# Last attention tiles reordered, the slots' second half skipped between narrow experts, and a copy in place of a dummy scatter

## The reference, cut to what matters

```python
u = rms_norm(h, norm1_g)
proj = u @ w_in
conv_out = conformer_conv_group(proj[..., :c0], conv_w, conv_b, conv_ln_g, conv_ln_b)
attn_out = swa_sink_attention(q, k, v, q_norm_g, k_norm_g, sinks)
h = h + concatenate([conv_out, attn_out], axis=-1) @ w_out
v = rms_norm(h, norm2_g).reshape(B * S, D)
h = h + moe_top4_of_32(v)      # sum of gate * (clamped_swiglu(v @ w1 + b1) @ w2 + b2)
```

## Time and profile before

| what | value |
|---|---|
| median of 3 runs | 1993.06 us (1991.5 to 1994.81) |
| profiled execution, its own time | 1994.85 us |
| its span in the trace | 1993.1 us |
| mean granted TensorE clock | 0.992 |
| PE busy | 1925.4 us, 97% of the span |
| DVE busy | 1010.1 us, 51% |
| ACT busy | 449.9 us, 23% |
| POOL busy | 415.6 us, 21% |
| bytes moved by DMA | 513.21 MB, 258 GB/s |

### The profile page before, as it was taken

How to read it: one execution, slowest core, us unless ns; L and a number is a source line. 1 busy time by engine, 2 the same in 40 slices (tenths; PEclk the granted TensorE clock), 3 DMA queues, 4 the chain that set the end, 5 groups by cost and what they waited for, 6 DMA issues and landing times.

```text
span 1993.1 us, 35237 instructions
## 1 busy us (share of the span) xinstructions
PE 1925.4 (97%) x12983; PEld 1589.3 (80%) x12984; DVE 1010.1 (51%) x2627; ACT 449.9 (23%) x983; POOL 415.6 (21%) x410
## 2 busy tenths in 40 slices
PE   5999989989999999999999999999999999999996
PEld 3545545457888877888887888999999999999996
DVE  2989973354555545555554555444444444443332
ACT  3166565111111111111111111222222211211111
POOL 3111100011222222222232222222222222221211
PEclk9999999999999999999999999999999999999998
DMA  7000033538999999999999999999888899887651
GB/s 242 1 1 1 6 112 136 186 114 293 349 343 332 352 338 350 351 341 332 351 339 351 351 347 331 313 323 311 303 301 302 304 308 308 298 294 244 223 181 40
DMA packets 237153, 513.21 MB, mean 258 GB/s; under 512 B 11085, under 2 KB 15721, under 8 KB 237104
## 3 DMA queue, kind: packets, MB, share of 16 engines
q1 hardware_dynamic: 215408, 448.89, 62.6%
q0 software_dynamic: 19840, 63.23, 11.9%
q10 hardware_dynamic: 1856, 0.41, 0.1%
HBM read 479.30 MB, written 33.19 MB: 257 GB/s over the span
## 4 chain that ended last, share of the span: by engine, by line
PE 91%; DVE 4%; ACT 2%; issue 1%; DMA 1%; POOL 0%; SPq 0%; ACTq 0%; DVEq 0%; POOLq 0%
PE bank L1175 50%; PE bank L1219 12%; PE bank L1194 12%; PE bank L1392 5%; PE bank L1267 4%; DVE arena L932 2%; PE bank L1303 2%; PE bank L1314 1%; PE bank L1207 1%; PE bank L1553 1%; PE bank L1208 1%; PE bank L1342 1%; DMA arena<-in_x 1%; PE bank L1259 0%; PE bank L1366 0%
## 5 line engine op out<-in xcount | busy, mean ns | idle before, releaser
L1175 PE MATMUL bank<-arena 128*128 128x128 f32 (+5 forms) x8192 | 1000.7, 284 | 6.9 <-issue 6.1
L1175 PEld LDWEIGHTS bank<-arena 128*128 128x128 f32 x8192 | 986.5, 191 | 18.8 <-issue 17.8
L377 POOL DMA_INDIRECT arena<-token_rows,idx_q x256 | 250.1, 977 | 649.0 <-PE bank L1175 589.1
L808 DVE TENSOR_SCALAR arena<-bank,b1c 128x256 f32<-128x256 f32 x256 | 123.4, 482 | 407.2 <-PE bank L1175 407.2
L497 ACT ACTIVATE arena<-arena 128x256 f32<-128x256 f32 x256 | 106.6, 417 | 853.9 <-DVE arena L808 853.9
L1219 PE MATMUL bank<-arena 128*128 128x512 f32 x576 | 250.2, 592 | 0.0
L1194 PE MATMUL bank<-arena 128*128 128x144 f32 (+4 forms) x1792 | 246.8, 293 | 3.0 <-ACT arena L501 2.9
L1194 PEld LDWEIGHTS bank<-arena 128*128 128x128 f32 x1792 | 235.3, 190 | 6.2 <-ACT arena L501 6.2
L383 POOL DMA_INDIRECT out<-arena,idx_cur x64 | 99.4, 1553 | 535.9 <-DVE arena L865 492.1
L1219 PEld LDWEIGHTS bank<-arena 128*128 128x128 f32 x576 | 108.1, 190 | 129.1 <-issue 129.1
L932 DVE SCALAR_TENSOR_TENSOR arena<-arena,cols 128x512 f32<-128x512 f32 (+1 forms) x226 | 182.3, 807 | 12.5 <-ACT arena L592 5.5
(11 more groups left out here) (229 smaller groups left out, 1102.4 us busy)
## 6 DMA issues: line engine op xcount, KB each, us to landing
arena<-in_w SPq DMA_DIRECT2D x192, 2048.0 KB, 12.6
arena<-in_b SPq DMA_DIRECT2D x32, 512.0 KB, 12.7
arena<-in_x SPq DMA_DIRECT2D x16, 512.0 KB, 6.4
token_rows<-arena SPq DMA_DIRECT2D x8, 576.0 KB, 3.2
out<-arena SPq DMA_DIRECT2D x8, 512.0 KB, 6.0
arena<-token_rows,idx_q POOLq DMA_INDIRECT x256
arena<-in_w_in SPq DMA_DIRECT2D x2, 1536.0 KB, 13.1
arena<-in_w_in SPq DMA_DIRECT2D x1, 3072.0 KB, 19.5
```

What stands on the lines that cost most here:

```text
L377: pool.indirect_dma_start(out=gath_q[:, g, :], out_offset=None, in_=quads_d, in_offset=bass.IndirectOffsetOnAxis(ap=idx_q[:, g:g + 1], axis=0)
L808: v.tensor_scalar(g1[:, r, :], bank[r][:, 0:SLOTS], b1c[:, m:m + 1], LIMIT, ALU.add, ALU.min).then_inc(g1_ready, 1)
L1175: last = mm(bank[m % 2][:, side * SLOTS:side * SLOTS + n], w1_sb[:, k, lo:lo + P], xT[:, k, 0:n], start=k == 0, stop=k == KD - 1)
```

## The change

**VectorE and ScalarE, last attention tiles.** In tile 6 the groups of taps go from 8, 4 and (behind the q normalization) 4 to 5, 7 and 0; the four taps taken away stay for the end, so the last group has nine taps and not five. In tile 7 `deviation(0)` goes from ahead of `softmax_a(6)` to behind the two-count group of taps, and `rescale(0)` from ahead of `softmax_b(6)` to behind it. Behind the last tile `softmax_b(7)` goes ahead of `deviation(1)`. ScalarE does `take_PT(6)` ahead of `swish(0)`, and `take_PT(7)` ahead of `swish(1)` in round t = 0 where it was in round 1.

**TensorE, last attention tiles.** In tile 7 `trans_q(7)` goes ahead of two of the four variance sums and two of the three mean sums; the second side of `out_half(0, 0)` goes behind `trans_p(6)`; `trans_p(7)` goes ahead of `turn_rows(0)` and `out_half(1, 1)`, with its wait on bank 5 changed from `vt_ev` to `cen_done`; `turn_rows(0)` side 1 gets a wait for `take_PT(7)`.

**Expert passes.** Where this pass and the next are narrow, `slots_to_tokens` does one half only. For that the narrow body is there twice on TensorE: a loop over 17 passes with one half and one pass with two. The codes move from bank 6 to bank 2 behind column 256. The second half of the codes keeps its earlier value, and the gathers still run by it. In a narrow pass the dummy indirect add on POOL becomes a plain DMA of 2 x 16 floats to a scratch tensor.

```diff
 # POOL, end of a pass
                 with pool.If(over < 1):
-                    add_rows(pool, 1, zeros)
+                    pool.dma_start(spare_d, zeros[:, 0:QW]).then_inc(added[1], 16)
 # ScalarE
                 if s + 1 < NT:
                     take_q(s + 1)
-                else:
-                    swish(0)
                 if s >= 1:
                     take_PT(s - 1)
+                if s == NT - 1:
+                    swish(0)
...
                 if t == 1:
-                    take_PT(NT - 1)
                     take_o(NT - 1)
...
                 if t == 0:
                     normalize(NT - 1)
+                    take_PT(NT - 1)
                     swish(1)
 # VectorE
-                if s == NT - 1:
-                    deviation(0)
                 if s >= 1:
                     softmax_a(s - 1)
                 if s == NT - 1:
                     some_taps(2, blocks)
-                    rescale(0)
+                    deviation(0)
                 else:
-                    some_taps(4, blocks)
+                    some_taps(2.5 if s == NT - 2 else 4, blocks)
                 if s >= 1:
                     softmax_b(s - 1)
+                if s == NT - 1:
+                    rescale(0)
                 if s == NT - 2:
-                    some_taps(2, blocks)
+                    some_taps(3.5, blocks)
                     center(0)
...
                     norm_qk(s + 1, blocks)
-                    some_taps(2 if s == NT - 2 else 4, blocks)
+                    if s < NT - 2:
+                        some_taps(4, blocks)
...
                 if t == 0:
+                    softmax_b(NT - 1)
                     deviation(1)
-                    softmax_b(NT - 1)
 # TensorE
                 if s == NT - 1:
-                    pe.wait_ge(vt_ev, 2)
+                    pe.wait_ge(cen_done, 2 * CT)
...
                 if s == NT - 1:
-                    for t in range(NT // 2):
-                        var_sum(0, t)
-                        if t < CT - 1:
-                            mean_sum(1, t, t + 1)
+                    var_sum(0, 0)
+                    mean_sum(1, 0, 1)
+                    var_sum(0, 1)
                 trans_q(s)
+                if s == NT - 1:
+                    mean_sum(1, 1, 2)
+                    var_sum(0, 2)
+                    mean_sum(1, 2, 3)
+                    var_sum(0, 3)
...
                     out_half(0, 0, (0,), range(2, CT))
-                    out_half(0, 0, (1,))
                 if s >= 1:
                     trans_p(s - 1)
+                if s == NT - 1:
+                    out_half(0, 0, (1,))
...
+                    if u == 0 and b == 1:
+                        pe.wait_ge(pt_ev, 3 * NT)
...
+                if t == 1:
+                    trans_p(NT - 1)
                 if t >= 1:
                     turn_rows(t - 1)
...
                 if t == 1:
-                    trans_p(NT - 1)
                     weigh_v(NT - 1)
...
-            def slots_to_tokens(n):
+            def slots_to_tokens(n, halves=2):
                 pe.wait_ge(oh_ready, n)
-                for h in range(2):
+                for h in range(halves):
...
-                        passes(length, n)
+                        if i > 0:
+                            passes(0, length, n, 2)
+                        else:
+                            with pe.If(length > 1):
+                                passes(1, length, n, 1)
+                            passes(0, 1, n, 2)
```

More of the change, by code:

```diff
@@ L52, in hybrid_block @@
     out2 = out.rearrange("b s d -> (b s) d")
+    QW = 16
+    spare_d = nc.dram_tensor("spare_rows", [2, QW], f32, kind="Internal").ap()
     rows_d = nc.dram_tensor("token_rows", [SEQ, ROW], f32, kind="Internal").ap()
@@ L783, in take_codes @@
         def take_codes(v):
-            return v.tensor_copy(idf[:], bank[6][:, 0:4])
+            return v.tensor_copy(idf[:], bank[2][:, SLOTS:SLOTS + 4])
         def take_idx(v, dst):
@@ L1159, in _, with pe_pass @@
                 dve_pass(v, q, e, e_next, prep, one_hots)
-        def pe_pass(pe, q, n, slots_to_tokens):
+        def pe_pass(pe, q, n, halves, slots_to_tokens):
             mm = pe.matmul
@@ L1179, in pe_pass @@
                 if m == 1:
-                    slots_to_tokens(q + 2)
+                    slots_to_tokens(q + 2, halves)
                 if m == 3:
@@ L1547, in _ @@
             keep_busy(6)
-            def slots_to_tokens(n):
+            def slots_to_tokens(n, halves=2):
                 pe.wait_ge(oh_ready, n)
-                for h in range(2):
+                for h in range(halves):
                     for t in range(NT):
-                        last = mm(bank[6][:, 2 * h:2 * h + 2], onehot[:, t, h * P:(h + 1) * P], tokcode[:, t, :],
+                        last = mm(bank[2][:, SLOTS + 2 * h:SLOTS + 2 * h + 2], onehot[:, t, h * P:(h + 1) * P], tokcode[:, t, :],
                                   start=t == 0, stop=t == NT - 1)
@@ L1586, in _, with passes @@
                 lap_base = pe.snap(lap * (len(WIDTHS) * P))
-                def passes(length, n):
-                    with pe.Fori(0, length):
+                def passes(begin, end, n, halves):
+                    with pe.Fori(begin, end):
                         q = pe.snap(done, min_val=0, max_val=QMAX - 1)
-                        pe_pass(pe, q, n, slots_to_tokens)
+                        pe_pass(pe, q, n, halves, slots_to_tokens)
                         pe.reg_add(done, done, 1)
```

## The result

The changed kernel took 1981.72 us (median of 4 runs, 1981.13 to 1983.63) beside 1993.38 us for the kernel before (4 runs); the ratio is 0.9944 with a 95% interval of 0.9927 to 0.9961. That is 11.7 us less, and the interval lies clear of 0.2%. The forecast was 1980.6. The profiled execution has a span of 1979.4 us where 1980.6 stood in the sum.

What follows compares the result with a forecast made beforehand. TensorE, carrying 91% of the span, was taken to bound the kernel. 9.3 us from the attention tiles and 3.2 from the slots, 12.5 off, gave a predicted median of 1980.6 us, range of 8 in 10 1977 to 1987.

Steps and rivals of the forecast that it cites:

- The slots: Narrow expert passes: eight small matmuls instead of sixteen save 0.19 us of TensorE's chain in 17 passes, 3.2 us.
- The doubled body: Second narrow loop body on TensorE and its branch: taken as zero cost, with 0.9 us in the range.
- The copy: Plain DMA for the dummy scatter on POOL, off TensorE's path with 5.4 us or more spare: zero either way.
- The second half of the tiles: Tile 7 after out_half(0, 1): net 1.45 us more, out_half(2, 0) at 323.6 instead of 332.90, 9.3 us in all.
- The first half of the tiles: Reordered tile 7 up to out_half(0, 1): that begins at 293.1 instead of 300.93, 7.8 us gained.
- I take full clock throughout: Attention tiles: TensorE's largest gap is 0.7 to 1.1 us; behind a 1.14 us gap work ran at full speed.
- Rival 1: Attention tiles: reordering gives only part, misplaced chains or a clock fall costing 3 to 6 us; 1983.6 to 1986.6; chance 0.19.
- Rival 3: Router: attention's gain is given back at another engine's wait, only the 3.2 us stay, 1989.9; chance 0.10.
- Rival 4: Narrow passes: the gather lands past its 1.7 us margin, each us costing 17 to 18 us, so slower; chance 0.05.
- Rival 2: Narrow passes: transfers bind at a share of 0.97, the 3.2 us are lost, 1983.8; chance 0.06.

Runs made afterwards that it cites:

- the expert part alone: Kernel before with only the one-half slots between narrow passes and the copy for the dummy scatter, attention tiles unchanged; ratio 0.9980 (0.9971 to 0.9989).
- the late part alone: Kernel before with only the last softmax sum, transposes and copies of tile 7's weights moved ahead; ratio 0.9998 (0.9989 to 1.0007).
- the overfilled kernel: Kernel before with 8 and 17 idle matmuls around the transposes of tile 6's weights, too long for the waits; ratio 1.0016 (1.0007 to 1.0025).
- The filled variant: Changed kernel with 3 and 5 idle matmuls in the waits of 0.69 and 1.25 us of tile 6; ratio 0.9946 (0.9933 to 0.9960).
- The tighter order: Changed kernel with take_o(5), take_o(6) earlier on ScalarE and TensorE's groups, attention products, spread(0) and out_half(0, 0) reordered further; ratio 0.9946 (0.9933 to 0.9960).
- the kernel before, filled: Kernel before with 4 and 8 idle matmuls in the two waits of tile 6; ratio 0.9999 (0.9990 to 1.0008).

## Why the prediction was right

**The slots.** Predicted 3.2 us, measured 3.4 in the traces (17 times 0.20: the eight that stay take 0.18 and not 0.19) and 4.0 (2.2 to 5.8) by the runs of the expert part alone. The doubled body costs no gap, as taken. By the Trainium skill (Runtime: NRT & Kernel Launch, Instruction fetch mechanics) a taken branch out of the fetched pages stalls for a fetch; at this branch TensorE has no gap in the trace. Whether a fetch is hidden there behind the matmuls is not shown.

**The copy.** Predicted zero, measured 0.9996 (0.9987 to 1.0005). It lands in 7.9 us, inside of the 6.3 to 9.8 of the scatter. The Trainium skill (DMA: Bandwidth & Descriptors, Anatomy of one DMA) fits the time of a DMA issued from POOL by 2.0 us plus a term for the bytes, an estimate of 2 us for 128 bytes. The measured 7.9 us is four times that, and decides.

**The second half of the tiles.** Predicted 1.45 us, measured 7.99 - 6.48 = 1.51, and 1.49 by the late part alone. The wait of side 1 of `turn_rows(0)` for `take_PT(7)` is there, as part of 1.41 us for eight transposes at 311.40.

**The first half of the tiles** is the term that was mis-sized: 7.8 predicted, 6.48 measured (51.08 less 44.60). The step that failed is that of the clock: "I take full clock throughout". I had compared the gaps one by one with one of 1.14 us behind which the clock stayed. That row was no safe measure: in the overfilled kernel the clock fell behind the same waits. In the changed kernel 0.69 us and then 1.25 us come close together, the clock falls behind them in all four of its traces that have them, and the seven groups with `trans_q(7)` take 10.0 us, 268.82 to 278.82. The second gap I had under-read too, as 1.1 us at most: `trans_p(5)` and `weigh_v(5)` come earlier and `take_o(5)` does not, so TensorE waits 1.25 us there where it waited 0.19. I had noted both facts, and put no wait on them. The wait itself costs nothing (the groups begin at K + 21.38, predicted K + 21.55); the fall behind it does.

The rows show the path of that price. The maximum was done at 274.37, as early as predicted (K + 26.93, predicted K + 26.95). But `trans_q(7)` ran at the lower clock, at K + 25.66 and not K + 24.85; ScalarE's copy of it stands ahead of the exponentials, so they began at 275.28, 0.9 us later than their maximum allowed. `normalize(6)` ended at 282.50, and TensorE, itself late, came to `trans_p(6)` at 282.77: K + 35.33 where K + 34.15 was predicted. These 1.18 us are nearly all of the missing 1.35 at `out_half(0, 1)` (K + 44.60, predicted K + 43.25). The filled variant has full clock and gets 0.65 us of them back, although its own filling holds `trans_q(7)` at K + 25.83. The tighter order, with full clock and no filling, has both points within 0.05 us of the prediction. It also has other edits, so it is no test of the clock alone. Rival 1 described this part; it came with 1.3 us instead of 3 to 6. The Trainium skill (TensorE: Matmul & The Clock Gate, A second HAM failure mode) tells of a kernel whose TensorE idles briefly between groups of matmuls, so often that its clock goes up and down. The falls here behind waits of 0.69 and 1.25 us agree with that in kind.

**Of the rest** the prediction had nothing, and it nearly cancels. The changed kernel gives 1.95 us back ahead of the first pass, since the clock falls at 420 to 427 us, and gets 1.6 back in the first pass, where the kernel before has its fall (the first 64 matmuls take 9.04 us there and 7.41 here). Rival 3, a give-back in the router, is this 1.95 and not 9. Rival 4 did not come: the transposes of the gathered rows still end 2.1 to 3.3 us ahead of TensorE's need in the narrow passes of the changed kernel. Rival 2 falls with the expert part alone: periods of 42.83 us.

**The total.** 8.0 + 3.4 = 11.4 by the stretches, 12.5 predicted, 11.7 and 11.1 by the medians of two sets of runs. The sum came out near for a part by luck, as the 1.95 lost and the 1.6 gained by falls of the clock, neither of them foreseen, nearly cancel. The nearness to 1980.6 of the profiled span of 1979.4 is luck too: it has 2.4 us from ahead of the change.

**Where the 8 us come from.** With full clock in the tiles of both, the stretch takes 80.82 us (the kernel before, filled) and 74.40 (the changed kernel, filled). So at least 6.4 of the 8.0 us are the order and its waits. By the filled runs the fall of the clock cost 2.2 us before and 0.7 in the changed kernel, which makes the other 1.6. By edit, the late part is 1.5 us and the taps of tile 6 are 1.7; the remaining 4.8, by difference, belong to the other edits of tile 7, which were not run apart. Whether the 2.2 us can be had as a gain in the total is doubtful: taken alone they were lost again behind. In the same way the attention change alone has 7.9 us in the tiles and only 4.2 (1.6 to 6.6) in the total. Why the clock falls more often behind a shorter stretch, or whether it does so by the timing of the execution alone, these runs don't settle; at 104 us and in tile 6 the same schedule had the fall in some executions and not in others.

## What to carry to other kernels

Walk a reordered schedule through engine by engine from the rows; it gave each start within 1.4 us, and the miss was a fall of the clock behind a wait whose cause had been seen but not followed up. Do not call a clock safe because one trace kept it behind a like wait. Neither the length of a wait nor the sum of several told it here: 1.96 us kept the clock in eight traces of 14; 1.14, 0.69 and 0.19 us kept the clock in seven traces, 1.14 and 0.69 lost it in one, and 0.69 and 1.25 us lost it in four of four. Give the clock a term in the range, with its price read from a stretch at the lower level. Where two orders differ by 1 or 2 us, compare stretches between fixed instructions in the traces, for falls of the clock elsewhere move the total by as much. An instruction on the bounding engine's path is worth its step in the chain (0.024 us here), not its recorded duration (0.163 us).

## What the runs showed of the hardware

The granted clock falls to its lower level (0.50) for some us in every one of the 14 traces, behind places where TensorE waits: at 104 us (behind 1.96 us, in 6 of 14), in the tiles, between 416 and 456 us. Filling one such place with idle matmuls kept the clock up there (K + 40.8 to K + 48.8 at 1.00) and the total stayed at 0.9999 (0.9990 to 1.0008): in the trace falls came later that had not been there. A plain DMA of 128 bytes issued from POOL took 1.18 us of the engine and 7.9 us to land, about as long as the dummy indirect add of two rows of 4 KB (1.36 us and 7.2 us for the one at 546.07 of the kernel before). Sixteen matmuls of two columns add 0.38 to 0.40 us to TensorE's chain, 24 to 25 ns for each, while the record of one shows 163 ns.
